# Two token tiles share one seven-product output projection in a two-layer diffusion backbone

## The chip, the cores and the metric

The kernel runs on one core of one Trainium2 chip. The metric is the device time of one launch in microseconds (us). Three runs of the kernel before gave 4073.3 us as their median (4071.96 to 4075.56).

TensorE (PE) multiplies matrices into PSUM, which has eight banks of 128 x 512 fp32 values. VectorE (DVE), ScalarE (ACT) and GpSimd (POOL) work on elements; SyncE (SP) issues most of the DMAs. Each engine runs its own program in order, and they wait for each other on semaphores.

## The reference, cut to what matters

```python
# h: modulated tokens; context 256 rows, latents 1024 rows; D_MODEL = 1024; DEPTH = 2
def merge(o_a, o_b, gates):
    g_a, g_b = jnp.split(gates, N_BRANCH, axis=-1)
    return (jax.nn.sigmoid(g_a) * (o_a @ w_oa) + jax.nn.sigmoid(g_b) * (o_b @ w_ob)) @ w_out

# in each layer, for the latents (and, in the first layer, for the context):
x = layer_norm(ALPHA * x + m[2] * y, ln1_g, ln1_b)          # y = merge(...)
h = modulate(x, m[3], m[4])
x = layer_norm(ALPHA * x + m[5] * ec_moe(h, ...), ln2_g, ln2_b)

def ec_moe(h, w_router, w_gate, w_up, w_down):
    aff = jax.nn.softmax((h @ w_router), axis=-1)           # 16 experts
    top_aff, top_idx = lax.top_k(jnp.swapaxes(aff, 1, 2), cap)
    # each expert: gather its rows, silu(x @ gate) * (x @ up) @ down, scatter-add
```

All data is fp32. The change is in the product `... @ w_out` and in what follows it until the experts start.

## The kernel before, in words

Each of the two layers runs the input projection, the attention of both branches, the merge (which leaves the gated sum in `mrgT`, transposed: eight k-chunks of 128 rows by 1280 tokens), then the **projection stage**, the choice of each expert's tokens, and sixteen experts. The change touches the projection stage and how the choice of tokens begins.

Tokens go in tiles of 128. Layer 0 has ten tiles (0 and 1 are context), layer 1 has the eight latent tiles 2 to 9. `TL[l]` is that list, `n` the place of a tile in it. For one tile:

- POOL copies the tile's eight chunks from `mrgT` to `mst`, four at a time (`take`, L2806).
- PE multiplies them with `w_o`: `y_half(t, 0)` takes chunks 0 to 3, `y_half(t, 1)` chunks 4 to 7, each with eight matmuls of 128 x 512, into banks 0 and 1 (L1188). A fp32 matmul shows as two records in the profile. After the second half comes `y`. The last tile is done by column half instead (`y_last`, L1265).
- DVE gates the row (`m2b`, L1890), which frees both banks (`y_used`), adds the residual row `xr` (L2269), takes its moments (L2277, L2281), and with ACT the inverse root. ACT writes the normalised row `xn` (L1703), DVE scales it with `gb1` to `x1t` (L1890, twice), ACT makes `zs` from it (L1721), and SP stores `x1t` to `x_mid` and `zs` to `moe_sum`.
- PE turns `xn` (`x1_transposes`, L768), ACT scales chunks 0 to 3 into `h2t` (`tr_a`, L1730), DVE chunks 4 to 7 (`tr_d`, L2319). Two tiles later in PE's program stand the router's sixteen small matmuls on `h2t` (`router`, L1215) between the halves, and `logits` (L1224).

In layer 0 DVE and ACT also do the context's choice of tokens, one step after each of the tiles 3 to 7 (`context_step`). At the end of the stage the last tile's logits take a short way (`rows_turned`, `ln_last`), then comes a softmax, and DVE's rounds of eight maxima (L2452, L2456). The first expert needs rows of `x_mid`, so POOL, once it has scaled the last tile's row (L2816, L2818) and all rows are stored, gathers them (L2829 context, L2835 latents). In layer 1 expert 0's latent row list is found first, by comparison (L2416 to L2437). Between these, PE runs short filler matmuls (`keep_clock`, L772).

SP orders its DMAs by hand. Expert weights go to a ring of twelve slots of 1 MB; slots 4 to 10 of expert 0 are loaded in the stage, one per tile, and 11, 0, 1, 2, 3, which lie under `w_o`, after the last `y`.

## Time and profile before

| what | value |
|---|---|
| median of three runs | 4073.3 us |
| the profiled execution | 4075.49 us, span 4073.8 us |
| PE busy | 3976.4 us, 98% of the span |
| DVE, ACT, POOL busy | 2049.3, 1072.4, 306.2 us |
| layer 0, projection stage | from 1181.4 to 1342.0 us of the span |
| layer 1, projection stage | from 3222.6 to 3351.0 us |
| layer 0, from there to expert 0's transposes | until 1386.8 us |
| layer 1, the same | until 3383.1 us |

A line of the profile names the line of the kernel, the engine, the operation, and what it writes and reads. "idle before" is the time in which that engine had nothing to do before the instruction, with what it waited for. The chain of waits follows the work that ended last from releaser to releaser.

### The profile page before, as it was taken

The numbers are of one execution on the slowest core, as the hardware profiler recorded it, in microseconds if no ns is written. First come the engines' busy times: TensorE is split into PE (matmuls) and PEld (weight loads), VectorE is DVE, ScalarE is ACT, GpSimd is POOL, SyncE is SP. The second block draws the span as 40 slices with busy tenths as digits, with TensorE's granted clock in tenths as the row PEclk, the third lists the DMA queues.
The fourth block names the chain that finished last, engine by engine and source line by source line (L and its number), as shares of the span: only waits on it lengthen the run. The fifth ranks groups of instructions, "written<-read, shape, count | busy, mean of one in ns | idle before, by whom it ended". The sixth has DMA issues, their size and how long they took to land.

```text
span 4073.8 us, 77692 instructions
## 1 busy us (share of the span) xinstructions
PE 3976.4 (98%) x31395; PEld 2860.4 (70%) x31396; DVE 2049.3 (50%) x4426; ACT 1072.4 (26%) x2422; POOL 306.2 (8%) x320
## 2 busy tenths in 40 slices
PE   8999999999999799999999999999999999999998
PEld 5565777655544688888888565777544448899997
DVE  1235766566645533333334444777544456444445
ACT  2335555400012111111111434555301121101013
POOL 0000000000000111111111000000000013110101
PEclk9999999999999899999999999999999999999999
DMA  6111000334334588888887221000333348999998
GB/s 220 60 55 61 19 19 19 104 109 119 114 118 151 171 266 265 271 270 266 265 266 225 84 79 55 19 19 19 94 109 89 120 174 254 325 330 326 330 326 280
DMA packets 558281, 658.02 MB, mean 162 GB/s; under 512 B 20014, under 2 KB 494860, under 8 KB 558092
## 3 DMA queue, kind: packets, MB, share of 16 engines
q1 hardware_dynamic: 526508, 564.10, 42.9%
q0 software_dynamic: 31008, 89.20, 7.7%
q8 instruction: 131, 2.15, 0.2%
q10 hardware_dynamic: 576, 2.10, 0.1%
q14 instruction: 58, 0.48, 0.0%
HBM read 582.92 MB, written 72.42 MB: 161 GB/s over the span
## 4 chain that ended last, share of the span: by engine, by line
PE 88%; DVE 5%; DVEq 2%; DMA 2%; SPq 1%; issue 1%; ACT 1%; POOL 0%; POOLq 0%; ACTq 0%
PE PS L764 36%; PE PS L1417 11%; PE PS L1448 9%; PE PS L768 8%; PE PS L997 7%; PE PS L1188 5%; PE PS L1068 3%; PE PS L902 2%; PE PS L1058 2%; DVE arena L1890 2%; PE PS L1442 1%; DVE arena L2165 1%; SPq L496 1%; PE PS L960 1%; DVEq L2169 1%
## 5 line engine op out<-in xcount | busy, mean ns | idle before, releaser
L764 PE MATMUL PS<-arena 128*128 128x160 f32 (+4 forms) x7004 | 1689.7, 402 | 12.6 <-DVE arena L1890 5.1
L764 PEld LDWEIGHTS PS<-arena 128*128 128x128 f32 x7004 | 1103.3, 190 | 570.6 <-issue 543.9
L1890 DVE TENSOR_TENSOR arena<-arena,PS 128x256 f32<-128x256 f32 (+3 forms) x661 | 290.8, 448 | 1032.3 <-ACT arena L1853 553.5
L1890 DVE TENSOR_TENSOR arena<-arena 128x1024 f32<-128x1024 f32 (+9 forms) x778 | 548.1, 722 | 132.3 <-PE PS L764 45.7
L768 PEld LDWEIGHTS PS<-arena 128*128 128x128 f32 (+1 forms) x2980 | 347.9, 142 | 197.5 <-issue 159.5
L768 PE MATMUL PS<-arena 128*128 128x128 f32 (+1 forms) x2980 | 436.6, 278 | 24.2 <-DMA arena<-x_mid,arena 14.9
L1417 PE MATMUL PS<-arena 128*64 128x128 f32 x8192 | 454.9, 273 | 1.6 <-DVE arena L1890 1.6
L1417 PEld LDWEIGHTS PS<-arena 128*64 128x64 f32 x8192 | 451.3, 137 | 5.1 <-DVE arena L1890 1.7
L1448 PE MATMUL PS<-arena 128*64 128x256 f32 x3600 | 396.0, 380 | 1.1 <-DVE arena L1890 0.5
L1853 ACT ACTIVATE arena<-PS 128x160 f32<-128x160 f32 (+1 forms) x256 | 74.7, 292 | 1176.5 <-PE PS L764 639.9
L1448 PEld LDWEIGHTS PS<-arena 128*64 128x64 f32 x3600 | 274.6, 137 | 117.1 <-issue 10.2
L997 PE MATMUL PS<-arena 128*128 128x512 f32 (+3 forms) x800 | 340.0, 520 | 8.7 <-ACT arena L1615 4.5
L2056 DVE TENSOR_REDUCE arena<-PS 128x1 f32<-128x512 f32 (+1 forms) x384 | 230.2, 600 | 60.1 <-PE PS L997 53.7
L1188 PE MATMUL PS<-arena 128*128 128x512 f32 x512 | 226.9, 597 | 5.8 <-DVE arena L1890 5.7
L1625 ACT ACTIVATE arena<-PS 128x512 f32<-128x512 f32 (+2 forms) x344 | 166.3, 503 | 233.0 <-PE PS L768 233.0
L1890 DVE TENSOR_TENSOR arena<-PS,arena 128x256 f32<-128x256 f32 (+7 forms) x275 | 105.7, 422 | 234.3 <-ACT arena L1633 105.0
L2165 DVE SCALAR_TENSOR_TENSOR arena<-arena 128x512 f32<-128x512 f32 x264 | 189.0, 749 | 13.8 <-DMA arena<-in_w_ada 2.6
L1615 ACT ACTIVATE arena<-PS,arena 128x1280 f32<-128x1280 f32 (+1 forms) x144 | 177.7, 1234 | 30.2 <-DVE arena L2058 25.2
L2066 DVE COPY arena<-PS 128x512 f32<-128x512 f32 (+2 forms) x256 | 155.9, 609 | 55.5 <-PE PS L768 55.3
L1188 PEld LDWEIGHTS PS<-arena 128*128 128x128 f32 x512 | 95.0, 190 | 120.7 <-issue 114.9
L1068 PE MATMUL PS<-arena 128*64 128x128 f32 x2624 | 155.8, 273 | 0.0
L997 PEld LDWEIGHTS PS<-arena 96*128 96x128 f32 (+1 forms) x800 | 126.5, 192 | 41.4 <-issue 30.8
(275 smaller groups left out, 2630.3 us busy)
## 6 DMA issues: line engine op xcount, KB each, us to landing
arena<-in_w_exp_gate SPq DMA_DIRECT2D x128, 1024.0 KB, 7.3
arena<-in_w_exp_up SPq DMA_DIRECT2D x128, 1024.0 KB, 9.7
arena<-in_w_exp_down SPq DMA_DIRECT2D x128, 1024.0 KB, 7.7
arena<-in_w_ada POOLq DMA_DIRECT2D x40, 1024.0 KB, 5.5
arena<-in_w_in SPq DMA_DIRECT2D x32, 512.0 KB, 5.5
h_transposed<-arena SPq DMA_DIRECT2D x20, 512.0 KB, 3.9
q_latent_attn<-arena SPq DMA_DIRECT2D x18, 512.0 KB, 2.8
arena<-q_latent_attn SPq DMA_DIRECT2D x18, 512.0 KB, 3.5
```

The lines of the kernel that those rows point to most:

```text
L764: m = pe.matmul(o, lt, rh, start=start and i == 0, stop=stop and i == n - 1)
L768: return pe.transpose(o, i, ident)
L997: pe.matmul(PS[:, b + i, 0:cn], qMt[0:rows, u, at_h, :], kT[0:rows, at_h, i * 512:i * 512 + cn], start=True, stop=True).then_inc(s["sM"], 1)
L1068: pe.matmul(PS[half(g), o, P:2 * P], V[:, kt, half(2 * c + g)], PT[:, place("AB"[g], n, kt), :], start=kt == 0, stop=kt == nm - 1)
L1188: m = pe.matmul(PS[:, h, :], (mst1 if isinstance(n, int) and n == 0 else mst)[:, k, :], w_o[:, k, h * 512:(h + 1) * 512], start=k == 0, st ...
L1417: m = pe.matmul(PS[g * 64:(g + 1) * 64, 3 + f % 2, h * N:(h + 1) * N], w[:, k, g * 64:(g + 1) * 64], xgT[:, k, 0:N], start=k == 0, stop=k ...
L1448: m = pe.matmul(PS[g * 64:(g + 1) * 64, b, c0:c0 + 256], lhs(k), rhs(g, k), start=start and k == 0, stop=stop and k == 3)
L1615: A(PM[:, g, 0:nk], flat(b)[:, 0:nk], ACT.Exp, bias=stat[:, st["negM"] + g:st["negM"] + g + 1], accum_out=stat[:, st["sums"] + 2 + g:st["s ...
L1625: A(PT[:, place(part, n, a0):place(part, n, a1), :].rearrange("p a b -> p (a b)"), turned(part, n, ci, a1 - a0), ACT.Copy).then_inc(s["pt_ ...
L1890: return dve.tensor_tensor(o, x, y, op)
L2056: dve.tensor_reduce(mxc[:, g, i:i + 1], PS[:, b + i, 0:min(512, TOK - i * 512)], AX.X, ALU.max)
L2165: m = dve.scalar_tensor_tensor(out=sums[:, v, :], in0=adB[:, h * 4 + k, :], scalar=silv[:, v, h * 4 + k:h * 4 + k + 1], in1=start, op0=ALU ...
```

## The change

The first two tiles of a layer are projected as before. The rest go in pairs (four pairs in layer 0, three in layer 1; `NPR`). A pair's 256 rows by 1024 chunks, and `w_o`, are each seen as 2 x 2 blocks, and the four result blocks are made with seven products of four matmuls of 128 x 512 (`product`), where two tiles took 32 matmuls. Operands that are sums are made by POOL: once a layer four sums of weight blocks (`weight_sum`, 2048 values per partition each), and four sums of row blocks per pair (`row_sums`, 512 values each). Three PSUM banks take the products in turn (`y_banks`); ACT copies the first product to SBUF (`P1s`), and DVE adds the products up, one column half of a row tile at a time.

The residual row and the row have two buffers each (`xrs`, `zta` beside `zt`). They and three of the weight sums lie in ring slots 7 to 10. So SP loads only slots 4 to 6 in the stage, and 8, 9, 10, 7 at the end, behind the rows of the last two tiles, which now stand behind the loads of 11, 0, 1, 2, 3. In layer 1 these also wait for the last DVE sum (`usum`). ACT takes chunks 4 to 7 of `h2t` too, except for the last tile but one.

```diff
+        WT1, WT2, WT4 = (at(R + 16384 + 2048 * i, 4, 512) for i in range(3))
+        W11, WT3 = w_o[:, 0:4, 512:1024], w_o[:, 0:4, 0:512]
+        W21, W22 = w_o[:, 4:8, 512:1024], w_o[:, 4:8, 0:512]
+        P1s, U1s, U2s, U3s = (mrgT[:, 2 * i:2 * i + 2, 0:CTX] for i in range(4))
+        xrs = xr, at(R + 14336, D)
+        zta = at(R + 15360, D)
+        def y_banks(q):
+            return ((5, 0, 1), (0, 1, 5), (1, 5, 0))[q % 3]
...
# SP
+                for n, t in enumerate(TL[l][:-2]):
+                    sp.wait_ge(*s("zs", n + 1))
+                    sp.wait_ge(*s("xr_in", 16 * (n + 2)))
+                    ld(xrs[n % 2], x_rows(l, t + 2), s["xr_in"])
+                    if n < 3:
                         ring_load(0, 4 + n)
+                    rows_out(t, n)
+                sp.wait_ge(*s("prod", 2 + 7 * NPR[l]))
+                if l:
+                    sp.wait_ge(*s("usum", 2 + 7 * NPR[l]))
+                    ld(fup, a["wmask"][:, 512:640], s["m_in"])
+                for c in (11, 0, 1, 2, 3):
+                    ring_load(0, c)
+                for n in (NT[l] - 2, NT[l] - 1):
+                    rows_out(TL[l][n], n)
+                sp.wait_ge(*s("lnn", NT[l] - 1))
+                for c in (8, 9, 10, 7):
+                    ring_load(0, c)
...
# PE
+                def y_pair(q):
+                    a, last = TL[l][2 + 2 * q], q == NPR[l] - 1
+                    X, Y, Z = y_banks(q)
...
+                    product(X, rows(a, 0), W11).then_inc(s["prod"], 1)
+                    x1_transposes(a - 2)
...
+                    product(Y, mst[:, 4:8, :], WT2).then_inc(s["prod"], 1)
...
+                    product(Z, mst[:, 0:4, :], WT1).then_inc(s["prod"], 1)
+                    router(a - 2)
+                    pe.wait_ge(*s("p1_cp", q + 1))
+                    product(X, rows(a, 1), W21).then_inc(s["prod"], 1)
+                    logits(a - 2)
+                    x1_transposes(a - 1)
...
+                    product(Y, mst1[:, 0:4, :], W22).then_inc(s["prod"], 1)
+                    if l == 0 and last:
+                        context()
...
+                    product(Z, mst1[:, 4:8, :], WT3).then_inc(s["prod"], 1)
+                    router(a - 1)
...
+                        m = product(X, rows(a + 1, 1), WT4)
+                    m.then_inc(s["prod"], 1)
+                    logits(a - 1)
...
# ACT
+                def pair_a(q):
+                    a, last = TL[l][2 + 2 * q], q == NPR[l] - 1
+                    root(a - 1)
+                    normal_rows(a - 1, zt)
+                    act.wait_ge(*s("prod", 7 * q + 3))
+                    A(P1s, PS[:, y_banks(q)[0], :].rearrange("p (a n) -> p a n", a=2), ACT.Copy).then_inc(s["p1_cp"], 1)
+                    tr_a(a - 2)
+                    scaled(a - 1)
...
# DVE, the second tile of a pair
+                    dve.wait_ge(*s("prod", 7 * q + 8))
+                    TTR(cut(zt[:, LO]), U3s, cut(PS[:, Z, :]), ALU.add).then_inc(s["usum"], 1)
+                    TTR(U2s, U1s, cut(PS[:, Z, :]), ALU.add).then_inc(s["usum"], 1)
+                    dve.drain()
+                    gate(zt, zt[:, LO], 0, LO)
+                    m = residual(n + 1, zt, LO, True)
...
+                    moments(zt, LO)
+                    if last:
+                        tr_d(a)
+                        x1_gain(a)
+                    else:
+                        x1_rows(a)
+                        if l == 0:
+                            context_step(a)
+                    dve.wait_ge(*s("prod", 7 * q + 9))
+                    TTR(cut(zt[:, HI]), U2s, cut(PS[:, X, :]), ALU.add).then_inc(s["usum"], 1)
...
# POOL
+                def row_sums(q):
...
+                    if q:
+                        pool.wait_ge(*s("prod", 7 * q - 2))
+                    pool.tensor_tensor(mst[:, 0:4, :], A21, A22, ALU.add).then_inc(s["mst"], 1)
+                    pool.drain()
+                    pool.tensor_tensor(mst[:, 4:8, :], mst[:, 0:4, :], A11, ALU.subtract).then_inc(s["mst"], 1)
+                    pool.drain()
+                    if q:
+                        pool.wait_ge(*s("prod", 7 * q + 1))
+                    pool.tensor_tensor(mst1[:, 0:4, :], A12, mst[:, 4:8, :], ALU.subtract).then_inc(s["mst"], 1)
+                    pool.tensor_tensor(mst1[:, 4:8, :], A11, A21, ALU.subtract).then_inc(s["mst"], 1)
```

PE before, one tile in the middle of layer 0's stage. L1188 are the projection's matmuls, L1215 the router, L1224 the logits, L768 the transposes:

```order
L1188 MATMUL PS<-arena 128x512 [waits y_used,mst]
L1188 MATMUL PS<-arena 128x512 x7
L1215 MATMUL PS<-arena 32x128 [waits rt_cp,h2d,h2a]
L1215 MATMUL PS<-arena 32x128 x7
L1188 MATMUL PS<-arena 128x512 [waits mst]
L1188 MATMUL PS<-arena 128x512 x7
L1224 MATMUL PS<-arena 128x16 [waits rt_cp]
L768 MATMUL PS<-arena 128x128 [waits h2d,h2a,lnn]
L768 MATMUL PS<-arena 128x128 x7
```

PE now, the first four products of a pair in the same place, without the first product's own rows. L1260 is `product`, L1228 the router, L1237 the logits, L780 the transposes:

```order
L1260 MATMUL PS<-arena 128x512 [waits mst,usum]
L1260 MATMUL PS<-arena 128x512 x3
L1260 MATMUL PS<-arena 128x512 [waits usum]
L1260 MATMUL PS<-arena 128x512 x3
L1228 MATMUL PS<-arena 32x128 [waits rt_cp,h2d,h2a]
L1228 MATMUL PS<-arena 32x128 x7
L1260 MATMUL PS<-arena 128x512 [waits p1_cp]
L1260 MATMUL PS<-arena 128x512 x3
L1237 MATMUL PS<-arena 128x16 [waits rt_cp]
L780 MATMUL PS<-arena 128x128 [waits h2d,h2a,lnn]
L780 MATMUL PS<-arena 128x128 x7
```

The router's tile is now the one whose transposes stand two products ahead of it in the same pair, and not a whole tile back.

ACT before, one tile: root (L1697), normalise (L1703), `zs` (L1721), logits copy (L1736), chunks 0 to 3 (L1730):

```order
L1721 ACTIVATE arena<-arena 128x1024 [waits z_st,x1]
L1736 ACTIVATE arena<-PS 128x128 [waits rt]
L1730 ACTIVATE arena<-PS,arena 128x128 [waits rt,x1T]
L1730 ACTIVATE arena<-PS,arena 128x128 x3
L1697 ACTIVATE arena<-arena 128x1 [waits lnv,x1T]
L1703 ACTIVATE arena<-arena 128x1024 [waits lnb]
```

ACT now, from the root of the pair before's second tile to `zs` (root L1720, normalise L1723, first product L1777, chunks L1757 and L1764, `zs` L1748):

```order
L1720 ACTIVATE arena<-arena 128x1 [waits lnv]
L1723 ACTIVATE arena<-arena 128x1024 [waits lnb,x1T]
L1777 ACTIVATE arena<-PS 128x2x256 [waits prod]
L1757 ACTIVATE arena<-PS,arena 128x128 [waits rt,x1T]
L1757 ACTIVATE arena<-PS,arena 128x128 x3
L1764 ACTIVATE arena<-PS,arena 128x128 [waits x1T]
L1764 ACTIVATE arena<-PS,arena 128x128 x3
L1748 ACTIVATE arena<-arena 128x1024 [waits z_st,x1]
```

The chunks of tile a - 2 now stand behind the normalisation of tile a - 1, where they stood ahead of it.

SP before, the end of the stage in layer 0:

```order
L496 DMA arena<-in_x 128x1024 [waits zs]
L496 DMA x_mid<-arena 128x1024 [waits x1]
L496 DMA moe_sum<-arena 128x1024 [waits z_set]
L496 DMA arena<-in_w_exp_down 128x8x256 [waits y]
L496 DMA arena<-in_w_exp_gate 128x8x256
L496 DMA arena<-in_w_exp_up 128x8x256
L496 DMA arena<-in_w_exp_gate 128x8x256
L496 DMA arena<-in_w_exp_up 128x8x256
L496 DMA x_mid<-arena 128x1024 [waits x1]
L496 DMA moe_sum<-arena 128x1024 [waits z_set]
```

SP now, in the same place:

```order
L511 DMA arena<-in_w_exp_down 128x8x256 [waits prod]
L511 DMA arena<-in_w_exp_gate 128x8x256
L511 DMA arena<-in_w_exp_up 128x8x256
L511 DMA arena<-in_w_exp_gate 128x8x256
L511 DMA arena<-in_w_exp_up 128x8x256
L511 DMA x_mid<-arena 128x1024 [waits x1]
L511 DMA moe_sum<-arena 128x1024 [waits z_set]
L511 DMA x_mid<-arena 128x1024 [waits x1]
L511 DMA moe_sum<-arena 128x1024 [waits z_set]
L511 DMA arena<-in_w_exp_down 128x8x256 [waits lnn]
L511 DMA arena<-in_w_exp_down 128x8x256 x2
L511 DMA arena<-in_w_exp_up 128x8x256
```

The rows of the last tile but one moved behind five weight loads, and four more loads stand behind the last tile's rows.

## Rows read from the trace of the kernel before

**Rows 1.** Layer 0's stage: window; length; busy PE, PEld, DVE, ACT, POOL; clock; DMA; GB/s:

```profile
1181.36:1342.02 160.66, 156.35 (x549) 73.74 (x548) 86.85 (x172) 43.14 (x79) 12.00 (x18) 1.00 0.45 154
```

**Rows 2.** Chain of waits (start us, us, what), both layers' stages:

```profile
1211.33 1.24 DVE arena L1890
...
1228.85 7.10 PE PS L1188 x16
1235.96 0.57 PE PS L1215 x16
...
1243.63 1.24 DVE arena L1890
1244.87 0.14 issue
...
3252.52 1.24 DVE arena L1890
```

**Rows 3.** PE in order of time (start us, us, what, idle before), one tile:

```profile
1243.57 1.07 PE L768 MATMUL PS<-arena 128*128 128x128 f32 x8
```

**Rows 4.** DVE in order of time, a tile's row work:

```profile
1247.63 0.21 DVE L2281 BATCH_NORM_AGGREGATE arena<-arena 128x2 f32<-128x12 f32 x1
...
1250.03 2.53 DVE L1890 TENSOR_TENSOR arena<-arena 128x1024 f32<-128x1024 f32 x2
```

**Rows 5.** ACT in order of time: normalising a row, a bank's copy, eight chunks:

```profile
1248.75 1.24 ACT L1703 ACTIVATE arena<-arena 128x1024 f32<-128x1024 f32 x1 [0.52 <-DVE arena L2290]
...
1342.45 0.60 ACT L1708 ACTIVATE arena<-PS 128x512 f32<-128x512 f32 x1 [6.49 <-PE PS L768]
...
3383.71 2.91 ACT L1806 ACTIVATE arena<-PS,arena 128x128 f32<-128x128 f32 x8 [5.00 <-PE PS L768]
```

**Rows 6.** Busy time by window, layer 0, a tile with a context step:

```profile
1277.00:1293.00 16.00, 15.86 (x60) 7.45 (x58) 11.03 (x25) 5.40 (x10) 1.33 (x2) 1.00 0.46 164
```

**Rows 7.** DVE in order of time, the last tile's end, layers 0 and 1:

```profile
1342.02 0.69 DVE L1890 TENSOR_TENSOR arena<-PS,arena 128x512 f32<-128x512 f32 x1 [5.29 <-PE PS L1265]
1342.80 0.69 DVE L2269 SCALAR_TENSOR_TENSOR arena<-arena 128x512 f32<-128x512 f32 x1
...
1346.25 0.29 DVE L2296 COPY arena<-PS 128x128 f32<-128x128 f32 x1 [0.34 <-PE PS L1215]
...
3351.01 0.69 DVE L1890 TENSOR_TENSOR arena<-PS,arena 128x512 f32<-128x512 f32 x1 [5.37 <-PE PS L1265]
```

**Rows 8.** POOL in order of time, the last row's scaling and the gathers:

```profile
1359.53 2.34 POOL L2818 TENSOR_TENSOR arena<-arena 128x1024 f32<-128x1024 f32 x1 [3.36 <-issue]
1366.59 1.05 POOL L2829 DMA_INDIRECT arena<-x_mid,arena  x1 [4.72 <-DMA moe_sum<-arena]
...
3362.78 2.34 POOL L2818 TENSOR_TENSOR arena<-arena 128x1024 f32<-128x1024 f32 x1 [1.87 <-issue]
3377.24 1.05 POOL L2835 DMA_INDIRECT arena<-x_mid,arena  x1 [12.13 <-DVE arena L2437]
```

**Rows 9.** Busy time by window, the end of the five weight loads:

```profile
1355.00:1360.00 5.00, 4.34 (x39) 4.15 (x38) 4.52 (x10) 0.00 (x0) 1.64 (x2) 1.00 0.76 244
3365.00:3370.00 5.00, 3.75 (x9) 1.19 (x11) 5.00 (x13) 1.06 (x1) 0.11 (x1) 0.50 1.08 384
```

**Rows 10.** DMA issues in layer 1 from 3360 to 3366 us (the last number: us to landing):

```profile
x_mid<-arena SPq DMA_DIRECT2D x1, 512.0 KB, 5.9
```

**Rows 11.** PE in order of time, between the stage and the first expert:

```profile
1369.99 6.46 PE L772 MATMUL PS<-arena 128*128 128x128 f32 x40
1378.63 0.33 PE L1358 MATMUL PS<-arena 128*32 128x32 f32 x16 [2.17 <-DVE arena L2466]
...
3383.07 1.04 PE L768 MATMUL PS<-arena 128*128 128x128 f32 x8
```

**Rows 12.** POOL in order of time, its copies beside idle and busy DVE:

```profile
1243.77 0.62 POOL L2806 COPY arena<-arena 128x512 f32 x1 [6.90 <-PE PS L1188]
...
1252.29 0.74 POOL L2806 COPY arena<-arena 128x512 f32 x1 [7.90 <-PE PS L1188]
```

More of the change, by code:

```diff
@@ L1256, in y_last, with product @@
-                def y_last(t):
-                    n = t - TL[l][0]
-                    for h in range(2):
-                        for k in range(KD):
-                            if h == 0 and k % 4 == 0:
-                                pe.wait_ge(*s("mst", 2 * n + k // 4 + 1))
-                            if h == 0 and k == 0:
-                                pe.wait_ge(*s("y_used", n))
-                            m = pe.matmul(PS[:, h, :], mst[:, k, :], w_o[:, k, h * 512:(h + 1) * 512], start=k == 0, stop=k == KD - 1)
-                        m.then_inc(s["y" if h else "y_mid"], 1)
-                        if h == 0:
-                            router(t - 2)
-                            x1_transposes(t - 1)
-                            logits(t - 2)
+                def product(bank, A, B, ks=range(4)):
+                    for k in ks:
+                        m = pe.matmul(PS[:, bank, :], A[:, k, :], B[:, k, :], start=k == 0, stop=k == 3)
+                    return m
@@ L1726, in tr_a @@
                     act.wait_ge(*s("x1T", 2 * n + 1))
-                    if not (isinstance(n, int) and n == 0):
+                    if n:
                         act.wait_ge(*s("rt", n))
@@ L1732, in tr_a @@
                     m.then_inc(s["h2a"], 1)
+                    if t == TT - 2:
+                        return
+                    act.wait_ge(*s("x1T", 2 * n + 2))
+                    for k in range(4, 8):
+                        m = A(h2t[:, k, :], PS[:, 3, (k - 4) * P:(k - 3) * P], ACT.Identity,
+                              scale=lng[:, v, 0, k:k + 1], bias=lng[:, v, 1, k:k + 1])
+                    m.then_inc(s["h2d"], 1)
                 def logits_a(t):
@@ L2280, in ln_d, with moments, variance, inverse @@
+                def moments(z, cols):
+                    dve.drain()
+                    for h in range(2):
+                        if cols.start <= h * 512 < cols.stop:
+                            dve.bn_stats(stat[:, 12 + 6 * h:18 + 6 * h], z[:, h * 512:(h + 1) * 512])
+                def variance():
                     dve.drain()
                     dve.bn_aggr(stat[:, 8:10], stat[:, 12:24]).then_inc(s["lnv"], 1)
-                    if last:
-                        first = SEQ // P - 1
-                        dve.wait_ge(*s("lg", n))
-                        dve.tensor_copy(lgs[:, 0:first, :].rearrange("p t e -> p (t e)"), PS[:, 7, TC * E:(TT - 1) * E])
-                        dve.tensor_copy(total, PS[:, 7, 256:256 + 2 * E])
+                def inverse(n):
```

327 lines of the change are left out of this document (181 added, 146 removed).

## The prediction, made before the change was run

> **What bounds the kernel now.** I read the busy times by window first. In layer 0's projection stage PE is busy 156.35 of 160.66 us at full granted clock, DVE 86.85, ACT 43.14, POOL 12.00 [rows 1]. PE sets the pace, and time can be won there only by giving PE less to do, as long as the others keep up. The chain of waits says the same: one tile is a half of 7.10 us, the router 0.57, the other half, then DVE's gate 1.24 and 0.14 of issue, 16.15 us from 1228.85 to 1245.0 [rows 2]. In that last 1.38 PE is not idle: the logits and eight transposes (1.07, from 1243.57) run in it until 1244.6 [rows 3]. So its true idle time is about 0.4 us a tile. Then I read what stands between the stage and the first expert, because there PE waits for a list from DVE and for gathered rows, which come by SP, POOL and the DMA queues [rows 7 to 11]. The change touches all of these.
>
> **What PE saves.** A product is half of a half-tile's eight matmuls, 7.10 / 2 = 3.55 us [rows 2]. A pair takes 7 x 3.55 = 24.85, two routers 1.14, and two sets of logits and transposes at about 1.2, which nothing hides any more, since three banks in turn let PE go straight on. That is 28.4 us against 2 x 16.15 = 32.3: 3.9 us less. By stages: in layer 0 the time from tile 1's last matmul to the last tile's is 1342.02 - 1211.33 = 130.7 us, in layer 1 3351.01 - 3252.52 = 98.5 [rows 2, 7]. With the change it is 4 x 28.4 in layer 0 and 3 x 28.4 in layer 1, plus a third set of transposes in the last pair (1.1) and the small context and total matmuls, which I estimate at 0.8 and 0.3: 115.5 and 86.6. **Gain 15.2 + 11.9 = 27.1 us**, if nobody is late.
>
> **Who is late within a pair.** Call the end of the pair before 0. PE wants the router of tile a - 2 at 3 x 3.55 + 1.07 = 11.7. ACT must have scaled that tile's eight chunks by then, but they stand in its program behind the normalisation of tile a - 1, which needs the last product of the pair before. DVE's part: a half-row operation takes 0.78 from start to start (1342.02 to 1342.80) [rows 7]. The fifth product ended 7.6 before 0 (two products and a router). DVE does four half-row operations for it (3.1) and takes the statistics, 1.12 until ACT normalises (1247.63 to 1248.75) [rows 4, 5]: -3.4. Five operations on the next product follow (3.9), then the earlier row's scaling (2.6) [rows 4]: DVE comes to the seventh product at +3.1. Four operations and 1.1 more: ACT normalises at 7.3, until 8.6, copies the first product (0.60) and scales eight chunks (2.91) [rows 5]: 12.1. PE waits 0.4 us per turn of pairs. In layer 0 context steps stand in that chain: one makes DVE busy 11.03 us in 16 [rows 6], where the whole stage has a mean of 8.7 [rows 1], so 2.4 to 3.1 more. I take 0.4 for four of the five turns and 3.0 for the last in layer 0. **Loss 4.6 us.** DVE itself, with seven more additions but fewer chunks to scale, has about 22 us of work in a pair of 28.4. POOL's row sums are ordered two products ahead and are hidden; at half of a 1024-value operation (2.34) [rows 8] each takes 1.2.
>
> **POOL beside DVE.** POOL's copy of 512 values took 0.62 us at 1243.77, beside a DVE gate that reads PSUM, and 0.74 at 1252.29, beside the tail of a row scaling with two SBUF inputs (1250.03 to 1252.56) [rows 4, 12]. So there is some exclusion, between 0 and one operation's length. POOL now has four sums per pair, 28 in all; two of four fall among DVE's two-input operations. From 0 to 14 x 1.2 = 17 us of delay for DVE, most of it where DVE has slack. I take 0.24 per turn: **loss 1.2 us**. The Trainium skill (SBUF — State Buffer, "SBUF: two separate sides") holds that the pair of ports is an exclusive lock, taken for the whole instruction, also against a DVE operation with two SBUF inputs. That speaks against sums on GpSimd; taken whole it is the third case below.
>
> **The end of the stage.** Here the change costs, in three steps.
>
> First DVE. When the last product ends, DVE still works on the earlier row (five operations, one set of four chunks, one scaling: about 1.4 late), then it adds before it gates (0.8), and an `x1t` addition (1.3) now stands ahead of the last row's inverse. Before, the last projection matmul and the copy of the router's result were 4.2 us apart (1342.02 to 1346.25) [rows 7]. I expect 7.2: **3.0 later in both layers**.
>
> Then the rows. The store of the last tile but one stands behind five 1 MB loads. Before, these were done at about +17 in layer 0 (the DMA moved 244 GB/s from 1355 to 1360, so until about 1358.6) and ran until 3370 (+19) in layer 1 [rows 9]. POOL may not touch the last row until that store lands, at +18.5. Its two operations with the gap between take 2.34 + 3.36 + 2.34 = 8.0 in layer 0 and 6.6 in layer 1 [rows 8]. So in layer 0 the row is ready at +26.5, the context gather starts 4.7 later at +31.2 (before: 1366.59, +24.6), and PE's transposes and fillers, which then took 3.4 to begin and 6.46 [rows 11], end at +41.1. DVE's list is ready at 36.6 + 3.0 = +39.6 (before: 1378.63, +36.6). PE is 1.5 to 2.5 behind it. **Layer 0's end costs 5.0 us.**
>
> In layer 1 the loads wait for DVE's last sum, 2.3 later: they end at +21.3, the store lands at +22, POOL ends at +28.7, and with 1.1 for `zs` and 3 for its store the latent gather starts at +33, where it was at 3377.24, +26.2 [rows 8]. It also meets the four loads that stand behind the last row. A store that had loads ahead of it took 5.9 us to land [rows 10]; I take 2 us more for the gather, from bounds 0 and 4. PE was at the transposes at 3383.07, +32.1, right behind its fillers [rows 11], so nothing of this is covered. 6.8 + 2 less some slack of the landing: **layer 1's end costs 7.5 us**. The expert that follows reads slot 7 only at its seventh column block, over 50 us after the stage, and the load lands at about +43: covered by 10 us.
>
> The sum: -27.1 + 4.6 + 1.2 + 5.0 + 7.5 = **-8.8 us**. From the profiled execution that is 4066.7 us; it stood 2.2 above the median, so the same step from the median gives **4064.5 us**.
>
> The Trainium skill (DMA: Bandwidth & Descriptors, "Queues, rings and completion order") says that a DMA engine goes round-robin between its queues packet by packet, while one queue's own descriptors go in order. By it the store waits for all five loads, and the gather shares with the four: the 7.5 us would stand.
>
> **The rivals.** A measurement of this kernel can tell about 0.2%, 8.1 us, from no change, so faster means below 4065.2 and slower above 4081.4.
>
> 1. The forecast, with terms off by some us each way: 4064.5, from 4058 to 4071. For it: each step has a row. Chance 0.45; about 0.27 of it lies below 4065.2.
> 2. The rows at the end are not late enough to matter: POOL's gap of 3.36 or 1.87 was code, not work, the gather lands as fast as before, and only DVE's 3.0 counts twice. Then 27.1 - 4.6 - 6.0 = 16.5: 4057, down to 4051 if the turns wait for nothing. Against it: fillers end where the gather lands. Chance 0.18.
> 3. The port lock at full size: POOL's and DVE's two-input operations exclude each other, DVE is 1.2 later in each of five turns twice over, and so is each router: about 8 us more than I took, 4072. Chance 0.17. With it I count the case in which a product costs more than half of a half-tile (each change of operand and bank breaks the flow by 0.12, 49 products: 6 us), the change then not doing all it says: 4070, chance 0.08.
> 4. Slower: the chain DVE, ACT, router becomes the bound of the pair. PE's 28.4 is met as long as ACT is done at 11.7; I have it at 12.1. From 3.9 us above that the gain is gone, and each further us costs seven. It would come from additions that read PSUM and a strided SBUF view: if a half-row operation took 1.3 instead of 0.78, thirteen of them stand in the chain, 6.8 us a turn. Over five turns that is 34 us more, partly covered, and with the ends the kernel would be at about 4085. Against it: gates that read PSUM run at 0.69 for 512 values [rows 7]. Chance 0.12.
>
> **How the numbers follow.** Faster: 0.27 + 0.18 and a little of 3, 0.46. Slower: 0.12. Same: 0.42. The range leaves out the better end of case 2 and most of case 4: 4053 to 4080.
>
> **What would show it.** Right: 28 matmuls per pair at 3.5 to 3.6 us a product; routers that wait for ACT, briefly, and longest in layer 0's last pair; in layer 1 a latent gather 6 to 8 us later against the last product than before, and PE idle ahead of the first transposes. Wrong: a PE that waits for `usum` or for POOL's sums within a pair (case 3 or 4), a gather at its old distance (case 2), or a DVE that is busy above 25 us in 28.

## The result and the profile after

| | before | after |
|---|---|---|
| median, us | 4073.4 (4071.2 to 4077.5, 20 runs) | 4081.7 (4078.3 to 4091.7, 20 runs) |
| span of the profiled execution, us | 4073.8 | 4077.6 |
| ratio of the times, with 95% interval | | 1.0022 (1.0015 to 1.0029) |

The change costs 8.3 us where a gain of 8.8 was forecast; the measured time lies just above the range. The two profiled spans differ by 3.8 us only, since that execution of the changed kernel is at the fast end of its runs (4079.3) and that of the kernel before 2.1 us above its median. So 4.5 us of the 8.3 lie in no trace, and what follows accounts for the 3.8.

I cut both traces at the same events of PE: the first matmul of tile 0 of the stage, the end of tile 1's last matmul, the end of the last product (before: of the last projection matmul), and the first of the eight transposes for expert 0. In us:

| stretch | layer 0 before | after | layer 1 before | after | difference |
|---|---|---|---|---|---|
| tiles 0 and 1 | 29.9 | 38.4 | 29.6 | 36.7 | +15.6 |
| pairs | 130.7 | 116.6 | 98.5 | 85.1 | -27.5 |
| end, to expert 0 | 44.8 | 51.6 | 32.1 | 43.2 | +17.9 |

That is +6.0 us. The stage began 1.1 us later, the time between the two stages is the same within 0.2 us, and what follows layer 1's stage took 3.4 us less in this execution, which gives the 3.8 of the spans. Those 3.4 I do not put down to the change: in the runs below the same stretch took from 687.4 to 690.8 us with no edit in it. So the pairs gave more than forecast, and two things took it back: the ends, which were forecast in kind, and a stretch at the start that the prediction never looked at.

**The start.** PE in order of time in the changed kernel (start us, us, line, operation, in brackets the idle time ahead and what ended it); L1200 is tile 0 and then tile 1:

```profile
1182.49 13.94 PE L1200 MATMUL PS<-arena 128*128 128x512 f32 x32
1205.10 15.76 PE L1200 MATMUL PS<-arena 128*128 128x512 f32 x32 [8.67 <-DVE arena L1931]
...
3225.29 14.00 PE L1200 MATMUL PS<-arena 128*128 128x512 f32 x32
3246.17 15.80 PE L1200 MATMUL PS<-arena 128*128 128x512 f32 x32 [6.88 <-DVE arena L1931]
```

The same places in the kernel before:

```profile
1181.43 13.94 PE L1188 MATMUL PS<-arena 128*128 128x512 f32 x32
1197.32 13.97 PE L1188 MATMUL PS<-arena 128*128 128x512 f32 x32 [1.95 <-DVE arena L1890]
```

PE waits for DVE's gate of tile 0, which frees the banks. Why was DVE late? POOL and then DVE of the changed kernel in that stretch:

```profile
1186.66 4.50 POOL L2922 TENSOR_TENSOR arena<-arena 128x2048 f32<-128x2048 f32 x1
1194.52 4.50 POOL L2922 TENSOR_TENSOR arena<-arena 128x2048 f32<-128x2048 f32 x1 [3.37 <-issue]
1199.18 4.55 POOL L2922 TENSOR_TENSOR arena<-arena 128x2048 f32<-128x2048 f32 x1 [0.16 <-issue]
```

```profile
1185.58 5.60 DVE L1931 TENSOR_TENSOR arena<-arena 128x8 f32<-128x8 f32 x6
...
1195.64 3.73 DVE L1931 TENSOR_TENSOR arena<-arena 128x128 f32<-128x128 f32 x2
1199.45 0.64 DVE L2296 TENSOR_REDUCE arena<-arena 128x16 f32<-128x128 f32 x2
1200.01 3.81 DVE L2443 COPY arena<-arena 128x128 f32<-128x128 f32 x1
1203.74 1.21 DVE L1931 TENSOR_TENSOR arena<-PS,arena 128x1024 f32<-128x1024 f32 x1
```

Three times a group of tiny DVE operations ends where a weight sum of POOL ends: 1191.18 and 1191.16, 1199.37 and 1199.02 (the end of the second of two operations), 1203.82 and 1203.73. The six operations of 128x8 take 1.43 us and the two of 128x128 0.49 us where POOL is idle (a later kernel's rows, below); the copy took 0.22 us in the kernel before and takes 3.81 here. While POOL works, they stand still: it is no slower stream but a full stop, of up to 3.6 us for one operation. The Trainium skill (SBUF — State Buffer, "SBUF: two separate sides") says of the port pair that these two engines share: it is an exclusive lock, which whichever of them starts first keeps for its whole instruction. This trace agrees, with those three ends. A second cost hangs on it: after 8.67 us of idleness the granted clock of PE was lower:

```profile
1205.10:1220.69 15.59, 15.59 (x33) 6.83 (x33) 5.50 (x8) 3.87 (x4) 0.00 (x0) 0.88 0.50 169
```

(window; length; busy PE, PEld, DVE, ACT, POOL; clock; DMA; GB/s). Tile 1 took 15.76 us and not 13.97, in layer 1 15.80 and not 13.98. Of the 15.6 us, 12.0 are PE's longer wait and 3.6 the lower clock behind it.

**The pairs.** The waits of PE in the pairs, layer 0, then layer 1 (line, releaser: total us, times, longest):

```profile
PE PS L1228 <- issue: 3.6, 3, 2.7
...
PE PS L1228 <- issue: 0.8, 2, 0.5
```

L1228 is the router. Single waits are 0.23, 0.62 and 2.71 us in layer 0, 0.52 and 0.24 in layer 1. A product takes 3.5 us from start to start (the ends in the rows overlap with the next start):

```profile
1319.45 0.65 PE L1228 MATMUL PS<-arena 128*32 128x128 f32 x16 [2.71 <-issue]
1320.02 3.70 PE L1260 MATMUL PS<-arena 128*128 128x512 f32 x8
```

Here the clock stayed up behind the wait of 2.71. In four of the kernels below it did not, behind the same wait: the router then takes 1.08 us and the product 4.6 to 4.9, and layer 0's pairs 117.9 to 118.2 us and not 116.6. The rows of one of them, with both changes for the end:

```profile
1310.36 1.08 PE L1229 MATMUL PS<-arena 128*32 128x128 f32 x16 [2.71 <-issue]
1311.38 4.63 PE L1261 MATMUL PS<-arena 128*128 128x512 f32 x8
```

So about 1.4 us of what the pairs gained is this execution's luck.

**The ends.** POOL of the changed kernel (against [rows 8]), layers 0 and 1:

```profile
1357.16 2.35 POOL L2955 TENSOR_TENSOR arena<-arena 128x1024 f32<-128x1024 f32 x1 [53.43 <-DMA x_mid<-arena]
1359.64 2.34 POOL L2957 TENSOR_TENSOR arena<-arena 128x1024 f32<-128x1024 f32 x1
1367.35 1.05 POOL L2968 DMA_INDIRECT arena<-x_mid,arena  x1 [5.36 <-DMA moe_sum<-arena]
...
3368.66 3.92 POOL L2955 TENSOR_TENSOR arena<-arena 128x1024 f32<-128x1024 f32 x1 [52.16 <-DMA x_mid<-arena]
3372.72 3.93 POOL L2957 TENSOR_TENSOR arena<-arena 128x1024 f32<-128x1024 f32 x1
3382.06 1.05 POOL L2974 DMA_INDIRECT arena<-x_mid,arena  x1 [5.41 <-DMA moe_sum<-arena]
```

PE (against [rows 11]): the context gather's transposes, then expert 0's in layer 0, and expert 0's in layer 1:

```profile
1373.58 0.66 PE L780 MATMUL PS<-arena 128*128 128x128 f32 x2 [15.40 <-DMA arena<-x_mid,arena]
...
1389.03 1.97 PE L780 MATMUL PS<-arena 128*128 128x128 f32 x8 [4.70 <-DMA arena<-x_mid,arena]
...
3390.25 1.09 PE L780 MATMUL PS<-arena 128*128 128x128 f32 x8 [0.45 <-DMA arena<-x_mid,arena]
```

The store that POOL waits for was issued behind the five loads and took 10.0 us to land, in either layer (in layer 0 from 1347.03 to 1357.03, and POOL starts at 1357.16):

```profile
x_mid<-arena SPq DMA_DIRECT2D x1, 512.0 KB, 10.0
```

And the context gather flies beside the four late loads, where before little else moved. From the issue to the landing after, and from the issue to the first fillers behind the transposes before (window as above; the last two numbers are DMA share and GB/s):

```profile
1367.40:1373.50 6.10, 0.00 (x0) 0.00 (x0) 5.46 (x13) 0.00 (x0) 1.00 (x1) 0.50 1.09 359
```

```profile
1366.60:1370.00 3.40, 0.46 (x3) 0.49 (x3) 3.01 (x8) 0.00 (x0) 1.04 (x1) 0.50 0.14 39
```

Before, PE turned the gathered rows 2.95 us after the gather's start:

```profile
1369.54 0.66 PE L768 MATMUL PS<-arena 128*128 128x128 f32 x2 [10.20 <-DMA arena<-x_mid,arena]
```

In layer 1 the late rows cost in a second way. POOL's two operations on the last row now fall into DVE's search for expert 0's row list and hold it up; DVE after, then before:

```profile
3370.22 2.44 DVE L2534 TENSOR_SCALAR arena<-arena 128x128 bf16<-128x128 f32 x1
...
3373.24 4.49 DVE L1931 TENSOR_TENSOR arena<-arena 128x1024 f32<-128x1024 f32 x2
```

```profile
3370.27 0.28 DVE L2418 TENSOR_SCALAR arena<-arena 128x128 bf16<-128x128 f32 x1
...
3371.13 2.52 DVE L1890 TENSOR_TENSOR arena<-arena 128x1024 f32<-128x1024 f32 x2
```

That is 4.1 us more, and the list is ready 33.8 us after the last product, only 1.2 ahead of the gather.

### The profile page after: what moved, and what is told of

It reads as the page before. It is cut to its first block, busy times and chain, and to the rows that moved or that the text cites. A ratio compares the mean times of both kernels' runs of the same rounds, so it can differ in the third digit from the quotient of the medians.

```text
span 4077.6 us, 77599 instructions
## 1 busy us (share of the span) xinstructions
PE 3957.0 (97%) x31339; PEld 2855.2 (70%) x31340; DVE 2097.7 (51%) x4443; ACT 1092.3 (27%) x2485; POOL 363.4 (9%) x328
## 4 chain that ended last, share of the span: by engine, by line
PE 87%; DVE 4%; DMA 3%; SPq 2%; DVEq 2%; issue 1%; ACT 1%; POOL 0%; POOLq 0%; ACTq 0%
PE PS L776 36%; PE PS L1443 11%; PE PS L1474 9%; PE PS L780 8%; PE PS L1009 7%; PE PS L1260 4%; PE PS L1080 3%; PE PS L914 2%; PE PS L1070 2%; SPq L511 2%; DVE arena L1931 2%; PE PS L1468 1%; PE PS L972 1%; DVE arena L2206 1%; DVEq L2210 1%
## 5 line engine op out<-in xcount | busy, mean ns | idle before, releaser
L776 PEld LDWEIGHTS PS<-arena 128*128 128x128 f32 x7004 | 1102.3, 190 | 569.7 <-issue 542.8
L1931 DVE TENSOR_TENSOR arena<-arena,PS 128x512 f32<-128x512 f32 (+4 forms) x710 | 323.3, 464 | 1056.2 <-ACT arena L1894 547.5
L1931 DVE TENSOR_TENSOR arena<-arena 128x1024 f32<-128x1024 f32 (+10 forms) x806 | 590.9, 749 | 148.6 <-PE PS L776 45.8
L780 PEld LDWEIGHTS PS<-arena 128*128 128x128 f32 (+1 forms) x2980 | 347.6, 141 | 211.0 <-issue 166.4
L780 PE MATMUL PS<-arena 128*128 128x128 f32 (+1 forms) x2980 | 436.3, 278 | 35.5 <-DMA arena<-x_mid,arena 20.9
L1443 PEld LDWEIGHTS PS<-arena 128*64 128x64 f32 x8192 | 448.8, 137 | 3.6 <-DVE arena L1931 2.0
L1474 PEld LDWEIGHTS PS<-arena 128*64 128x64 f32 x3600 | 274.6, 137 | 117.0 <-issue 9.9
L1260 PE MATMUL PS<-arena 128*128 128x512 f32 x392 | 176.5, 598 | 0.0
L1931 DVE TENSOR_TENSOR arena<-PS,arena 128x256 f32<-128x256 f32 (+6 forms) x259 | 87.9, 378 | 153.8 <-ACT arena L1659 105.4
L1080 PEld LDWEIGHTS PS<-arena 128*64 128x64 f32 x2624 | 145.7, 137 | 0.6
```

The costliest lines, as they stand in the source:

```text
L776: m = pe.matmul(o, lt, rh, start=start and i == 0, stop=stop and i == n - 1)
L780: return pe.transpose(o, i, ident)
L1080: pe.matmul(PS[half(g), o, P:2 * P], V[:, kt, half(2 * c + g)], PT[:, place("AB"[g], n, kt), :], start=kt == 0, stop=kt == nm - 1)
L1260: m = pe.matmul(PS[:, bank, :], A[:, k, :], B[:, k, :], start=k == 0, stop=k == 3)
L1443: m = pe.matmul(PS[g * 64:(g + 1) * 64, 3 + f % 2, h * N:(h + 1) * N], w[:, k, g * 64:(g + 1) * 64], xgT[:, k, 0:N], start=k == 0, stop=k ...
L1474: m = pe.matmul(PS[g * 64:(g + 1) * 64, b, c0:c0 + 256], lhs(k), rhs(g, k), start=start and k == 0, stop=stop and k == 3)
```

## Experiments

The theory after the first look: **P**, POOL's weight sums stop DVE at the stage's start and that costs about 15 us; against it **D**, the start is late for some other reason of the new program. For the ends: the store behind the loads, or the loads that run beside the gather, or DVE's list.

### The weight sums, cut short

```
-                    pool.tensor_tensor(o, x, y, ALU.subtract)
+                    pool.tensor_tensor(o[:, :, 0:2], x[:, :, 0:2], y[:, :, 0:2], ALU.subtract)
```

> The changed kernel with each weight sum made over 2 of 512 columns only (so the projection's result is not the reference's); every wait and every other instruction stays. Theory P (ports): POOL's three weight sums of 4.5 us each hold DVE's setup operations and so tile 0's gate, and PE starts tile 1 22.6 us after tile 0 in layer 0 and 21.1 in layer 1, where it was 15.9 and 15.7 before. It expects 15.9 and 15.7 again here, and about 14 us less in all than the changed kernel (around 4064 to 4067). Rival D (DMA): the router's weights or the residual rows come later because of SP's new order of loads; then tile 1's start stays at about 22 and the time at 4080. The pairs should take the same 116.6 us in layer 0 by both, less some 1 us by theory P.

Measured: 4064.7 us (4063.8 to 4067.3, 8 runs), ratio to before 0.9979 (0.9967 to 0.9990). PE at tile 1:

```profile
1197.81 13.97 PE L1200 MATMUL PS<-arena 128*128 128x512 f32 x32 [2.18 <-DVE arena L1931]
```

The start is back at the old length (1181.70 to 1197.81), in layer 1 too (15.4), and 17 us are gone. P holds, D falls (the sums are incomplete here, so this kernel is only a measurement). In the pairs PE waits for the router 3.6 and 0.8 us in all, as before the edit: the weight sums' cost lies in the start alone.

### The same sums in the kernel before

```
                 take(tl + 1)
...
+                pool.wait_ge(*s("wo_in", 16))
+                for o, x, y in ((w1, wb, wa), (w2, wd, w1), (w4, wc, w2)):
+                    pool.tensor_tensor(o, x, y, ALU.subtract)
+                    pool.drain()
```

> The kernel before, with nothing of the change but the first three weight sums on POOL, in the same place, their results unused. Theory P expects tile 1's start at 21 to 23 us after tile 0's in both layers (15.9 and 15.7 before) and 11 to 14 us more in all, about 4086. Rival D expects no change from 4073, since SP's order is the old one.

Measured: 4093.4 us (4090.4 to 4094.2, 4 runs), ratio 1.0043 (1.0023 to 1.0063): 19.6 us slower, with none of the seven products in it. PE at tile 1:

```profile
1204.61 15.72 PE L1188 MATMUL PS<-arena 128*128 128x512 f32 x32 [8.65 <-DVE arena L1890]
```

The idle time is that of the changed kernel to 0.02 us. The two stages with their ends took 9.2 and 7.2 us more than before, close to the 8.5 and 7.1 at the changed kernel's start. The whole costs more than the 11 to 14 us expected: 4.0 us more lie between the stages and 2.4 less behind them, for which I have no cause.

### The sums on DVE, where it waits anyway

Between 1191.2 and 1195.4 DVE of the changed kernel waits for the router's weights. Here it makes the three sums there (POOL's fourth, of WT3, stays).

```
 (DVE, ahead of its wait for the router's weights)
+                dve.wait_ge(*s("wo_in", 16))
+                TTR(WT1, WT3, W11, ALU.subtract)
+                dve.drain()
+                TTR(WT2, W22, WT1, ALU.subtract)
+                dve.drain()
+                TTR(WT4, W21, WT2, ALU.subtract).then_inc(s["wo_in"], 1)
 (POOL)
-                weight_sum(WT1, WT3, W11)
-                weight_sum(WT2, W22, WT1)
-                weight_sum(WT4, W21, WT2)
+                pool.wait_ge(*s("wo_in", 17))
...
```

> The changed kernel with the three first weight sums on DVE, in the 8 us in which it waits for the router's weights, instead of on POOL (the result is the reference's). Each should take about 2.2 us, 6.7 in all, hidden in that wait. Theory P expects tile 1's start back at 16 us after tile 0's and 13 to 14 us less than the changed kernel, around 4067. Rival D expects 4081 or more, since DVE has more to do.

Measured: 4065.3 us (4062.6 to 4070.4, 8 runs), ratio 0.9981 (0.9970 to 0.9992): 16 us less than the changed kernel, and faster than the one before. DVE:

```profile
1184.69 1.43 DVE L1931 TENSOR_TENSOR arena<-arena 128x8 f32<-128x8 f32 x6
...
1186.22 7.02 DVE L1931 TENSOR_TENSOR arena<-arena 128x2048 f32<-128x2048 f32 x3
1195.09 0.17 DVE L2294 MEMSET arena<- 128x128 f32 x1 [1.85 <-DMA arena<-in_w_router]
...
1195.36 0.49 DVE L1931 TENSOR_TENSOR arena<-arena 128x128 f32<-128x128 f32 x2
```

A sum takes DVE 2.34 us where POOL takes 4.50, all three fit ahead of the weights that DVE waits for, and 1.85 us of the wait is still left. Tile 1 starts 16.4 us after tile 0. What remains of the change's cost is at the ends: 51.9 us in layer 0, 41.9 in layer 1. All kernels below but the next one build on this one.

### Rows by ACT's queue, alone

On the changed kernel: ACT, which makes `zs`, also issues the stores of the last two tiles' rows, so that they don't stand behind SP's five loads. SP's four late loads still run then.

```
 (SP)
-                for n in (NT[l] - 2, NT[l] - 1):
-                    rows_out(TL[l][n], n)
+                sp.wait_ge(*s("zs", NT[l]))
 (ACT)
+                def rows_stored(t):
+                    n = t - TL[l][0]
+                    act.wait_ge(*s("x1", n + 1))
+                    act.dma_start(x1_d[ds(t * P, P), :], x1t).then_inc(s["x1_st"], 16)
+                    act.wait_ge(*s("z_set", n + 1))
+                    act.dma_start(z_d[ds(t * P, P), :], zs).then_inc(s["z_st"], 16)
...
                 scaled(TT - 2)
+                rows_stored(TT - 2)
...
                 scaled(TT - 1)
+                rows_stored(TT - 1)
```

> The changed kernel with the rows of the last two tiles stored by ACT's DMA queue and not by SP's behind the five weight loads; SP's four late loads wait for the last residual instead. Theory Q (queue): the end of a stage is long because the store of the last tile but one stands in SP's queue behind five 1 MB loads, POOL waits for it, and everything to the gather follows. From the last product to expert 0's transposes it took 51.6 us in layer 0 and 40.9 in layer 1 (44.7 and 32.1 before); theory Q expects about 47.5 and 35 here, 9 to 10 us less in all, around 4072. Rival V (DVE): the end is long because DVE is late for the last product and adds before it gates, and the queue is covered; it expects less than 2 us of gain. Rival G (gather): the loads slow the gather; since nine loads now run without a gap until 27 us after the last product and the gathers come after that, it expects the gather's landing back at 4.9 us but POOL's start as late as now.

Measured: 4077.4 us (4075.8 to 4083.9, 8 runs), ratio 1.0012 (1.0000 to 1.0023). About 4 us, not 9 or 10. (The changed kernel's end in layer 1, against which this is to be read, is 43.2 us long, as in the table, and not 40.9.) POOL, layer 0:

```profile
1352.04 2.35 POOL L2962 TENSOR_TENSOR arena<-arena 128x1024 f32<-128x1024 f32 x1 [49.07 <-ACT arena L1722]
...
1366.18 1.05 POOL L2975 DMA_INDIRECT arena<-x_mid,arena  x1 [9.29 <-DMA moe_sum<-arena]
```

Against the last product POOL starts 4.4 us sooner, but then it waits 9.29 us for the last store, not 5.36: beside it the nine loads now run without a gap. So the gather starts only 0.4 us sooner, and the end takes 50.2 us (51.6). In layer 1 the gather starts 4.3 us sooner and the end takes 38.8 (43.2). There POOL's two operations are done before DVE's search reaches the place shown above, they take 2.34 us each, the list is ready 4.0 us sooner, and it is the list that the gather waits for:

```profile
3376.41 1.05 POOL L2981 DMA_INDIRECT arena<-x_mid,arena  x1 [12.13 <-DVE arena L2560]
```

Getting out of the queue was half of the remedy.

### The four late loads, alone

On the kernel with the sums on DVE; the rows stay in SP's queue. In layer 0 two loads of 8 KB (`mod_rows`), which stood behind the four, now go ahead of them.

```
                 sp.wait_ge(*s("lnn", NT[l] - 1))
+                sp.wait_ge(*s("gat", 16))
                 for c in (8, 9, 10, 7):
                     ring_load(0, c)
```

> On top of the kernel whose weight sums run on DVE (4065.3 us): only the four expert loads behind the last rows wait until expert 0's gather has landed; the rows stay in SP's queue, behind the five loads. Moving both had given 4054.8. Theory B (both halves count, the loads by sharing the DMA engines with the last row's store and the gather): the two-operation stretch of POOL starts where it did (1348.6 in layer 0, 3353.7 in layer 1), but the context gather is landed 3 us after its issue, not 6, until DVE's list is what PE waits for (it was ready 4.4 us ahead of PE), and the latent gather of layer 1 some 3 us sooner: 4 to 7 us in all, 4058 to 4061. Theory Q (only the queue behind the five loads counts, the four late loads cost nothing): 4064 to 4066. Theory L (only the late loads count, the queue costs nothing): 4054 to 4056.

Measured: 4061.0 us (4058.6 to 4068.2, 7 runs), ratio 0.9969 (0.9957 to 0.9980). The interval overlaps with that of the kernel it builds on, so the times alone don't show the gain; the median fits theory B, and the trace shows its mechanism. The gather in layer 0 took 2.8 us to land, in layer 1 4.5; before the edit 6.0 and 7.6:

```profile
1364.69 1.05 POOL L2977 DMA_INDIRECT arena<-x_mid,arena  x1 [4.70 <-DMA moe_sum<-arena]
```

POOL starts on the row 20.4 us after the last product, 20.0 without the edit: the queue is as it was. The ends are 47.7 and 38.9 us long, 4.2 and 3.0 less.

### Both together

The edits of the last two sections together, on the kernel with the sums on DVE.

> On top of the kernel with the weight sums on DVE (4065.3 us): the rows of the last two tiles go by ACT's queue, and the four late weight loads wait until expert 0's latent rows are gathered. Theory Q says that the loads delay the end twice: the stores stand behind five of them, and the stores and gathers share the engines with the other four. With the stores by ACT alone the last store of layer 0 still took 7.4 us to land, beside nine loads. Expected here: last product to expert 0's transposes about 46 us in layer 0 and 34 in layer 1 (51 and 41 with SP), the last stores landing in 3 us and the gather in 4.9 and under 5.8; about 4055 to 4058. A rival, that the first expert then waits for its late slots, expects PE idle in expert 0's seventh block or down products, and no gain.

Measured: 4054.8 us (4053.4 to 4055.2, 3 runs), ratio **0.9953** (0.9937 to 0.9969): 18 us faster than the kernel before, and with the kernel of all edits (below) the fastest. PE at layer 0's end:

```profile
1357.56 0.66 PE L781 MATMUL PS<-arena 128*128 128x128 f32 x2 [7.18 <-DMA arena<-x_mid,arena]
...
1369.41 0.44 PE L1385 MATMUL PS<-arena 128*32 128x32 f32 x16 [5.31 <-DVE arena L2597]
```

The rows are there 5.3 us too early now; what ends last in layer 0 is DVE's list, 39.6 us after the last product. So layer 0's end is 48.5 us, no shorter than with the late loads alone, and the gain of the ACT queue is layer 1's: 36.0 us, 2.8 less than with the loads alone. There too the gather waits for DVE's list now (12.29 us, at 3358.72), and the list comes sooner than with the loads alone since POOL's operations hold it up less. Rows that come sooner than the list are worth nothing. Against the kernel before, the two ends are still 3.7 and 3.9 us longer; in layer 0 the list is 3.0 later, as forecast for DVE. No edit tested DVE's part by itself.

### Fillers where PE waits for the last row

```
                 router(TT - 2)
+                pe.wait_ge(*s("usum", 1 + 7 * NPR[l]))
+                keep_clock(5 if l else 0, 9)
```

> On top of the kernel with the weight sums on DVE (4065.3 us): nine filler matmuls in the 2.2 us in which PE waits for the last row's residual. PE's granted clock fell to half for a stretch behind that wait (the ten filler records took 2.38 us, 1.36 before the change). Theory C (clock): that stretch is on the path; the router and the fillers after it run at full speed again here, and each layer's end is 1 to 1.5 us shorter, 2 to 3 in all. Rival: DVE, which still has the last but one row's addition to do, is as late as PE, and the gain is under 0.5 us.

Measured: 4065.9 us (4063.1 to 4067.9, 8 runs), ratio 0.9981 (0.9971 to 0.9992): no gain. The ten fillers that follow take 1.36 us here and 2.26 without the edit, and the transposes that DVE's selection needs begin 1.0 us sooner after the last product (9.9 against 10.9). But at 4065 us layer 0's end hangs on rows and gather, which started 30.7 and 30.3 us after the last product. The clock was repaired where nobody waited for it.

### The context step later

In layer 0, DVE makes the context step behind the second tile's statistics instead of ahead.

```
                         x1_rows(a)
-                        if l == 0:
-                            context_step(a)
...
                     inverse(n + 1)
+                    if l == 0:
+                        context_step(a)
```

> On top of the kernel with the weight sums on DVE (4065.3 us): in layer 0 the context's step after the first tile of a pair is done behind the statistics of the second tile, and not ahead of them. The router of layer 0's last pair waited 2.71 us for ACT's chunks, the two before 0.23 and 0.62. If the chain DVE, ACT, router is what makes them late, the last wait falls to about 0.4 and the time by 2 to 2.5 us. If ACT itself were too slow, the wait stays.

Measured: 4066.2 us (4064.8 to 4070.6, 8 runs), ratio 0.9982 (0.9972 to 0.9993): no gain. PE in layer 0:

```profile
1276.08 0.38 PE L780 MATMUL PS<-arena 128*16 128x128 f32 x2 [3.15 <-DVE arena L1931]
1276.29 8.73 PE L1260 MATMUL PS<-arena 128*128 128x512 f32 x16
...
1312.99 0.65 PE L1228 MATMUL PS<-arena 128*32 128x128 f32 x16 [0.24 <-issue]
```

The router's wait of 2.71 is 0.24: the context step was its cause. It came back a pair earlier as 3.15, where PE's turning of a context row waits for DVE, and the two products behind it took 8.73 us instead of 7.03. The pairs are 118.5 us long, against 116.6 in the kernel this one builds on and 117.9 to 118.2 in those whose clock fell behind the wait of 2.71.

With all edits of this section at once (this one, the fillers, the rows and the loads):

> All at once: weight sums on DVE, rows by ACT's queue with the four loads after the gather, fillers in the last wait, the context's step behind the statistics. If the parts add up: 4065.3 - 8 - 2 - 2 = about 4053 us, 0.5% under the kernel before (4073.8). If the parts cover each other (the list of DVE becomes the end's bound), about 4057.

Measured: 4054.8 us (4054.4 to 4058.2, 4 runs), ratio 0.9956 (0.9939 to 0.9973), the same as with the rows and loads alone. In layer 0 DVE's list is ready at 38.4 us and not 39.6, and the end takes 46.8 us and not 48.5: where the list ends last, the fillers are worth about 1.2 us. Layer 1's end is 37.0 against 36.0 and layer 0's pairs are 0.5 longer, so that little of it is left.

### The row sums, cut short

The weight sums were POOL's at the start; do POOL's row sums in the pairs cost anything?

```
-                    pool.tensor_tensor(mst[:, 0:4, :], A21, A22, ALU.add)
+                    pool.tensor_tensor(mst[:, 0:4, 0:2], A21[:, :, 0:2], A22[:, :, 0:2], ALU.add)
 (and the other three likewise)
```

> On top of the kernel whose weight sums run on DVE (4065.3 us): each of POOL's row sums is made over 2 of its 128 rows of a tile's token columns, so that POOL holds nothing while the pairs run; the sums are incomplete, all matmuls, gates and gathers keep their sizes. That kernel's PE waits for the router in the pairs: 3.6 us in layer 0 (the longest 2.7) and 1.1 in layer 1. Theory A (those waits are POOL's row sums in DVE's way, the exclusion at full size): they go, 4 to 5 us less, 4060 to 4062. Theory W (they are DVE's and ACT's own work, with the context step in layer 0's last pair): they stay within 1 us, 4064 to 4066, and the 2.7 stays above 2.

Measured: 4068.7 us (4064.0 to 4073.2, 10 runs), ratio 0.9986 (0.9977 to 0.9996): no gain (a loss isn't shown: the interval overlaps with that of the kernel it builds on). PE's waits for the router, layer 0, then layer 1:

```profile
PE PS L1228 <- ACT arena L1764: 2.6, 1, 2.6
PE PS L1228 <- issue: 2.5, 2, 2.3
...
PE PS L1228 <- ACT arena L1764: 2.6, 1, 2.6
PE PS L1228 <- issue: 0.2, 1, 0.2
```

The long one of the last pair stays at 2.3 (theory W). The waits that were there fell from 3.6 to 2.5 us in layer 0 and from 1.1 to 0.2 in layer 1, so the row sums cost up to 2.0 us. That is hidden in the time, since a new wait of 2.6 us stands in the first pair of each layer, with a product of 5.38 us at a lower clock behind it in layer 0 (3.70 without). POOL:

```profile
1212.07 4.51 POOL L2928 TENSOR_TENSOR arena<-arena 128x2048 f32<-128x2048 f32 x1
```

With the row sums short, POOL's fourth weight sum starts 1.1 us after the end of tile 1 and not 6.3 behind it, as in the changed kernel (1227.16, after 1220.86). There it meets DVE's work on tile 1's row, an operation of 1.22 us otherwise:

```profile
1212.28 5.38 DVE L2315 SCALAR_TENSOR_TENSOR arena<-arena 128x1024 f32<-128x1024 f32 x1
```

The row comes 4.2 us late, and 2.6 of that reach the router. In the changed kernel the same sum stops DVE's two operations of 1024 values that scale the row (7.70 us for 2.5 of work), and PE waits for nothing: DVE had the time there. One operation of POOL, in two places.

## Why the prediction was wrong

**What PE saves, who is late within a pair:** right, and a little too careful. With its stalls it made the pairs 120.0 and 87.9 us; they took 116.6 and 85.1. PE's own work was 113.0 and 84.3 where 115.5 and 86.6 were forecast, and the rest are waits. The router's waits were forecast as 0.4 in four turns and 3.0 in the last of layer 0, and were 0.23, 0.62, 2.71, 0.52 and 0.24. The 3.0 was put down to the context step, and the kernel with that step later shows it. Gain after stalls: 21.3 forecast, 27.5 measured, of which 1.4 is the clock's luck named above.

**POOL beside DVE: the step that failed.** Its term was 1.2 us, and the start alone took 15.6. It counted the 28 row sums, which are short and meet little; they cost up to 2.0 us, not far from what it gave them. It left out the three weight sums of 4.5 us each, though the diff has them, and they lie in the one stretch where DVE has small chained operations and PE waits for the result. What would have been needed was in the trace of before: PE's idle 1.95 us ahead of tile 1, which says that DVE is already the last to be ready there, and POOL's 2.34 for 1024 values [rows 8], hence about 4.6 for 2048. Three of these are 14 us, put in front of a DVE that is last: that bounds the cost of a layer, and the measured 8.5 and 7.1 us in the two layers, the lower clock of tile 1 included, are within it. The third rival had the right mechanism, the lock at full size, but at the pairs and at 8 us. The fourth, on the slow side, did not happen: DVE, ACT and router did not become the bound.

**The end of the stage:** right in its mechanism, too small in its size. Layer 0 was put at 5.0 and took 6.8. POOL was to start at +18.5, and started at +19.7; the gap of 3.36 us between its two operations, which the sum kept, was 0.1; the context gather was to start at +31.2, and did so at +29.9; DVE's list was put at +39.6, and in the kernel whose rows come first it was ready at +39.6. The missed part is the gather's landing: 2.95 us before, while 39 GB/s moved, and 6.1 now, at 359. The prediction gave that sharing only to layer 1, although the four late loads stand behind the rows in both. Layer 1 was put at 7.5 and took 11.1: POOL started at +21.6 (+22 forecast), but its two operations took 3.92 and 3.93 where 2.34 each had been taken, and DVE's list was held up beside them by 4.1: the same exclusion once more, at a place where the prediction had no term for it. The gather started at +35.0 and not +33 and landed in 8.1.

**The sum.** -27.5 + 15.6 + 17.9 = +6.0 by the trace against -8.8. Without the start's 15.6 it would have been -9.6. The kernels without POOL's weight sums measured 4064.7 and 4065.3, close to the 4064.5 of the forecast, but that is in part luck: in the changed kernel the pairs were 6.2 better and the ends 5.4 worse than their terms.

## What to carry over

Before work goes to an idle engine, look at what runs beside it at the very place where it will stand, not at the stage's mean: three 4.5 us sums on POOL in each layer cost 16 us because a row of 0.2 us operations on DVE was on the path there, while 28 short ones elsewhere cost 2 us at most. Long one-time operations deserve more suspicion than the many short ones of a loop. And when the middle of a stage gets shorter, follow each store and load to the next stage: here 10.5 of the 27.5 us that the products saved were lost to a queue behind weight loads and to the loads beside it, and they came back in full only when both were changed.

## What the hardware did that I had not expected

- The exclusion hits both ways and also operations with one input: a DVE copy of 128x128 took 3.81 us instead of 0.22 beside POOL, a TENSOR_SCALAR of 128x128 2.44 instead of 0.28, and POOL's operation of 1024 values 3.92 instead of 2.34 beside DVE.
- The context gather of layer 0 landed in 2.8 to 2.9 us without the late loads and in about 6 beside them, the latent gather of layer 1 in 4.5 or 4.6 and in 7.6 to 8.1; a 512 KB store behind five loads of 1 MB took 10.0, and by another queue beside the loads 5.9 to 8.4.
- The granted clock after a wait of 2.4 us was 1.00 in one kernel (the sums on DVE: 2.43 us, tile 1 in 13.97) and 0.89 in another with nearly the same wait (the four late loads alone: 2.44 us), as the window shows:

```profile
1201.11:1216.78 15.67, 15.67 (x33) 6.91 (x34) 5.50 (x8) 3.87 (x4) 0.00 (x0) 0.89 0.58 202
```

  So one profiled execution can differ by 1.7 us at such a place without any edit, and by 1.4 us in layer 0's last pair, as said above.
